# Expert rows of a mixture-of-experts layer: one slot in memory each, or scatters that add into two sums per token

## The chip, the core and the metric

The kernel runs on one core of a Trainium2 chip. Five engines work side by side, each from its own instruction stream, and meet at semaphores: TensorE (PE in the rows; its weight loads are PEld), VectorE (DVE), ScalarE (ACT), GpSimd (POOL) and SyncE (SP), which here issues DMAs. Sixteen DMA engines move the data of all queues. The metric is the time of one execution on the device, in microseconds (us).

## What is computed

The reference is one layer of a streaming encoder for 320 tokens (256 of a new stream, 64 of a running one) with 1024 features, all in float32: a projection, three token mixers, a merge with layer norm, and then a mixture of experts with a second layer norm. The change lies in the mixture of experts:

```python
s = sigmoid(t @ w_router)                 # 320 tokens, 64 experts
eidx = top 8 of (s + router_bias), out of the 4 best of 8 groups
gates = s[eidx] / sum * 2.5
routed = sum over the 8 chosen e: gate * (silu(t @ w1[e]) * (t @ w3[e])) @ w2[e]
h = layer_norm(alpha * h + routed + shared)
```

Each token gets the sum of eight expert rows of 1024 numbers, so there are 320 * 8 = 2560 rows, 40 per expert on average.

## The kernel before

Earlier stages run first: the recurrent mixer (about 130 to 450 us of the span, where the unused DRAM rows of the experts are also cleared), the other mixers, merge, layer norm and routing, up to about 973 us. Then come the experts.

**Experts.** They are handled in 32 pairs (`NP`), experts 2n and 2n+1 in pair n. A pair has 128 rows: 64 places (`CAP`) for each of its two experts, of which about 40 hold a token. For each pair TensorE gathers the token rows by one-hot matrices (`gather`, two halves, L1036 and L1041), or for five of them (`FETCHED`: 6, 11, 16, 21, 26) turns rows that GpSimd has fetched from memory with an indirect DMA (L2352). Then come `hidden` (L1069, 32 matmuls), `turn` (L1077) and `down` (L1088, 16 matmuls). TensorE's order for pair n is: hidden(n), first half of the rows of n+1, turn(n), second half of the rows of n+1, down(n). If an expert had more than 64 tokens, a loop behind `more > 0` would take them; it doesn't run with these inputs.

**VectorE in a pair.** Its order is `hid_step(n)`; `x_step(n+1)`, which copies half of the gathered rows out (L2121) and the row's place (`IDX`); the one-hot matrices of pair n+2; and `y_step(n)` (L1496 on 128x512), which scales half of the expert's output by the gate into `Y`. ScalarE does the other half of each.

**The scatter.** GpSimd's `scatter(n)` waits for both halves of `Y`, issues one indirect DMA (L2340) that stores the 128 rows of 4 KB in DRAM, then waits until it has landed and adds one to `rows_out` (L2344). Only then does it go on to the next. `IDX` and `Y` have two buffers, so `x_step(n+2)` on VectorE waits until scatter n has landed. The row of a token's k-th chosen expert goes to a slot of its own: `slots` has 2560 rows, and a place without a token has an index beyond the end and is not stored. The slot comes from a scan over the chosen experts in the routing stage (`TRK`, L2039 and the lines behind it), which ends in `INFO`, a table of gate and place for each token and expert. The last two pairs (30 and 31) aren't scattered: TensorE adds them by one-hot matrices (`combine`, L1099).

**Weights.** SyncE loads 6.3 MB for each pair, into three slots used in turn. The up weights of pair n (L498, two of 2 MB) are issued when hidden(n-3) is done, the down weights (L501, two of 1 MB) when down(n-3) is.

**The end.** After scatter 29 has landed, SyncE loads all slots, five times 2 MB (L533, L542), over weights that are no longer needed. VectorE sums them (`sum_rows`: adds of 2048, 1024 and 1024 numbers per partition, L244, L246, L249, four times: three between its steps of the last two pairs, one after them). TensorE adds the remaining rows of the last 64 tokens with 16 matmuls (L1155). Then VectorE adds TensorE's sums (L1492), takes the statistics (L2200) and does the layer norm; SyncE stores the output.

## Time and profile before

| | |
|---|---|
| three runs | 1503.83, 1505.06, 1506.80 us |
| median | 1505.06 us |
| span of the profiled execution | 1502.1 us, 2.96 below the median |
| TensorE busy | 1457.5 us (97% of the span) |
| VectorE busy | 647.1 us (43%) |
| GpSimd busy | 116.8 us (8%) |
| DMA moved | 375.27 MB |

The span runs from the first to the last instruction of one execution; no other figure of that execution's time is shown. "Idle before <- X" in a row is time in which the engine waited, and X what ended it. "DMA to landing" is the time from the issue of a transfer to its last byte. Matmul ends are modelled, so matmul rows overlap a little.

### The profile page before, as it was taken

Reading aid. Unit: us, or ns where it says so; the run is one execution under the profiler, and the core shown is the slowest. Engines: PE = TensorE matmul, PEld = TensorE weight load, DVE = VectorE, ACT = ScalarE, POOL = GpSimd, SP = SyncE. Lnnn points to the kernel's source line nnn. Section 1 sums busy time; section 2 is a strip of 40 time slices with the busy share of each in tenths; the row PEclk is TensorE's granted clock in tenths of the full one; section 3 lists DMA queues with packets and bytes.
Section 4 is the critical chain, followed back from the end, with each engine's and each line's share of the span. In section 5 each row is a group of like instructions: output and inputs, shape, how many; then the busy total and the mean of one; then the engine's idle time right before and its main releaser. Section 6 shows DMA issues by size and latency. Waiting matters only on the chain.

```text
span 1502.1 us, 31068 instructions
## 1 busy us (share of the span) xinstructions
PE 1457.5 (97%) x13071; PEld 1011.2 (67%) x13071; DVE 647.1 (43%) x1227; ACT 390.4 (26%) x874; POOL 116.8 (8%) x107
## 2 busy tenths in 40 slices
PE   7999999999999999999999999999999999999995
PEld 6776667677776777767766765766666767675751
DVE  5223778875644677734541114622211112121228
ACT  2112444442322554435431011111111111111111
POOL 3000113121010000000000000000000001000000
PEclk9999999999999999999999999999999999999998
DMA  7778375563344544565577538689999999999985
GB/s 243 168 174 181 101 214 166 132 203 97 103 130 147 138 112 116 178 180 163 135 231 263 157 100 359 251 337 399 417 423 430 428 426 429 426 428 429 427 342 211
DMA packets 157017, 375.27 MB, mean 250 GB/s; under 512 B 101708, under 2 KB 110300, under 8 KB 139216
## 3 DMA queue, kind: packets, MB, share of 16 engines
q1 hardware_dynamic: 123712, 341.35, 63.9%
q10 hardware_dynamic: 26592, 15.49, 3.5%
q0 software_dynamic: 6576, 16.48, 3.2%
q8 instruction: 102, 1.67, 0.5%
q14 instruction: 35, 0.29, 0.1%
HBM read 327.14 MB, written 51.95 MB: 252 GB/s over the span
## 4 chain that ended last, share of the span: by engine, by line
PE 82%; DVE 7%; DMA 4%; ACT 2%; DVEq 2%; issue 1%; SPq 1%; ACTq 1%; POOLq 0%
PE PS L576 27%; PE PS L1069 14%; PE PS L919 8%; PE PS L1036 7%; PE PS L1088 6%; PE PS L624 4%; PE PS L1041 2%; PE PS L957 2%; DVE region L1492 2%; DVE region L1499 2%; PE PS L632 1%; ACT L1172 1%; PE PS L1052 1%; PE PS L1077 1%; PE PS L817 1%
## 5 line engine op out<-in xcount | busy, mean ns | idle before, releaser
L576 PE MATMUL PS<-h0T,region 128*128 128x320 f32 x1808 | 510.2, 437 | 1.0 <-issue 0.8
L576 PEld LDWEIGHTS PS<-h0T,region 128*128 128x128 f32 x1808 | 336.8, 190 | 144.6 <-issue 12.2
L1172 ACT ACTIVATE region<-PS 128x9 f32<-128x9 f32 (+6 forms) x407 | 148.5, 383 | 681.9 <-PE PS L576 311.8
L1069 PE MATMUL PS<-region 128*64 128x512 f32 x1024 | 228.8, 592 | 0.0
L1069 PEld LDWEIGHTS PS<-region 128*64 128x64 f32 x1024 | 124.5, 137 | 92.2 <-issue 31.9
L1492 DVE TENSOR_TENSOR region<-region 128x256 f32<-128x256 f32 (+10 forms) x210 | 127.0, 624 | 96.8 <-ACTq L1218 76.2
L919 PE MATMUL PS<-region 128*128 128x320 f32 x512 | 138.6, 433 | 1.3 <-DMA region<-wo 1.2
L919 PEld LDWEIGHTS PS<-region 128*128 128x128 f32 x512 | 97.0, 190 | 42.5 <-issue 1.7
L1172 ACT ACT_TABLE_LOAD x80 | 102.6, 1283 | 73.1 <-DMA region<-projected 56.7
L1088 PE MATMUL PS<-region,history 128*64 128x512 f32 x512 | 119.7, 596 | 1.0 <-ACTq L1454 0.7
L1172 ACT ACTIVATE region<-region 128x256 f32<-128x256 f32 (+8 forms) x160 | 81.2, 531 | 147.9 <-DMA region<-projected 37.0
L1036 PEld LDWEIGHTS PS<-region,h 128*128 128x128 f32 x864 | 100.6, 192 | 22.5 <-issue 22.4
L1036 PE MATMUL PS<-region,h 128*128 128x128 f32 x864 | 108.1, 278 | 0.4 <-issue 0.4
L1492 DVE TENSOR_TENSOR history<-region,PS 128x256 f32<-128x256 f32 x32 | 13.5, 421 | 200.4 <-ACTq L1449 200.3
L1492 DVE TENSOR_TENSOR region<-PS,region 128x1024 f32<-128x1024 f32 (+3 forms) x49 | 38.2, 807 | 123.1 <-PE PS L919 93.2
L2121 DVE COPY region<-PS 128x512 f32<-128x512 f32 x32 | 22.1, 692 | 157.2 <-PE PS L1052 76.1
L1088 PEld LDWEIGHTS PS<-region,history 128*64 128x64 f32 x512 | 56.1, 137 | 38.5 <-issue 13.7
L2340 POOL DMA_INDIRECT expert_rows<-region,row_index x25 | 24.4, 976 | 721.1 <-DVEq L2149 721.1
L1499 DVE SCALAR_TENSOR_TENSOR region<-region,feature_vectors 128x320 f32<-128x320 f32 (+1 forms) x103 | 65.9, 639 | 19.9 <-ACTq L285 8.3
L1172 ACT ACTIVATE region<-PS,region 128x512 f32<-128x512 f32 x33 | 22.7, 688 | 158.1 <-PE PS L1088 158.0
L624 PEld LDWEIGHTS PS<-region 64*64 64x64 f32 x2720 | 50.0, 134 | 19.1 <-issue 13.4
L624 PE MATMUL PS<-region 64*64 64x64 f32 (+1 forms) x2720 | 56.4, 227 | 6.1 <-DVEq L1690 2.7
(210 smaller groups left out, 1163.8 us busy)
## 6 DMA issues: line engine op xcount, KB each, us to landing
region<-moe_w SPq DMA_DIRECT2D x64, 2048.0 KB, 17.4
region<-moe_w SPq DMA_DIRECT2D x64, 1024.0 KB, 15.0
region<-w_in SPq DMA_DIRECT2D x115, 512.0 KB, 5.6
region<-wo SPq DMA_DIRECT2D x32, 512.0 KB, 3.6
projected<-region ACTq DMA_DIRECT2D x65, 167.5 KB, 3.9
expert_rows<-region SPq DMA_DIRECT2D x20, 512.0 KB, 7.2
region<-expert_rows SPq DMA_DIRECT2D x5, 2048.0 KB, 14.4
region<-projected SPq DMA_DIRECT2D x10, 768.0 KB, 6.3
```

The lines of the kernel that those rows point to most:

```text
L576: last = mm(PS[:, 6 + i % 2, 0:NTOK], WR[:, i, k, :], H0T[:, k, :], start=(k == 0), stop=(k == KT - 1))
L624: last = mm(head(out(j), 1 - x if across and j > 3 else x), head(lhs(j), x), head(rhs(j), x), **kw)
L919: last = mm(PS[:, b, 0:NTOK], WR[:, q, k, :], OT[:, 8 * q + k, :], start=(k == 0 and q < 3), stop=(k == KT - 1 and q != 2))
L957: last = mm(PS[:, 2 * t + h, :], MG[:, k, t * 128:t * 128 + 128], WOUT[:, k, h * 512:h * 512 + 512], start=(k == 0), stop=(k == KT - 1))
L1036: last = mm(bank(h, 4, 128)[:, k], H0[:, t, (4 * h + k) * 128:(4 * h + k) * 128 + 128], OH[:, p, t, :], start=(h == 0 and k == 0 and t == ...
L1041: last = mm(bank(g, 4, 128)[:, k], head(H0, g)[:, 2, (4 * g + k) * 128:(4 * g + k) * 128 + 128], head(OH, g)[:, p, 2, :], start=(g == 1 an ...
L1069: last = mm(PS[tiles(i), 2, :], XE[:, k, tiles(i)], W13[r][i][:, k * 512:k * 512 + 512], start=(k == 0), stop=(k == KT - 1))
L1088: last = mm(PS[tiles(i), 5 + h, :], HIDT[:, f, tiles(i)], W2[r][i][:, f * D + h * 512:f * D + h * 512 + 512], start=(f == 0), stop=(f == 1))
L1172: return nc.scalar.activation(out, in_, f, **kw)
L1492: return dve.tensor_tensor(out, a, b, op)
L1499: return dve.scalar_tensor_tensor(out=out, in0=a, scalar=s, in1=b, op0=op0, op1=op1)
L2340: pool.indirect_dma_start(slots[:, :], bass.IndirectOffsetOnAxis(ap=places, axis=0), Y[:, p, :], None, bounds_check=last_slot, oob_is_err= ...
```

## The change

The DRAM tensor of 2560 slots becomes one of 640 rows: two sums for each token. Experts with an even number go to row `token`, those with an odd number to row `320 + token`. The two experts of a pair thus never meet in a row within one scatter. Each scatter now has `compute_op=ALU.add`: it adds its rows to what stands there. Its place in the instruction streams and its waits stay.

- The 20 stores that clear the slots become 5, all issued behind the weights of the first step of the recurrent mixer.
- The routing stage no longer counts a token's chosen experts; the place is the token's number plus 0 or 320.
- At the end there are two loads of 1 MB and two of 256 KB; VectorE does two adds for each of three token tiles (`add_sums`: 1024 numbers per partition, and 512 in the last tile).
- TensorE's 16 matmuls of L1155 (eight in the program, each of which the trace shows twice) and their wait are gone.

```diff
-SLOTS = NTOK * TOPK
+SUMS = 2 * NTOK
...
-        slots = nc.dram_tensor("expert_rows", (SLOTS, D), FP32, kind="Internal").ap()
+        sums = nc.dram_tensor("expert_sums", (SUMS, D), FP32, kind="Internal").ap()
+        sums_of = sums.rearrange("(r n) d -> n r d", r=2)
...
-        def sum_rows(e, k):
-
-            t, w = k // 2, 128 if k < 4 else 64
-            rw = ROWS[k][0:w]
-            e.tensor_tensor(rw[:, 0:2], rw[:, 0:2], rw[:, 2:4], ALU.add)
-            e.drain()
-            e.tensor_tensor(rw[:, 0], rw[:, 0], rw[:, 1], ALU.add)
-            e.drain()
-            if t < 2:
-                e.tensor_tensor(ACC[:, t, :], ACC[:, t, :], rw[:, 0], ALU.add)
-            else:
-                e.tensor_copy(ROWS[k][64:128, 0, 0:512], rw[:, 0, 512:D])
+        def add_sums(e, t):
+
+            acc = ACC[:, t, :] if t < 2 else ACC[:, 2, 0:512]
+            for r in range(2):
+                e.tensor_tensor(acc, acc, ROWS[t][:, r], ALU.add)
                 e.drain()
-                e.tensor_tensor(ACC[:, 2, 0:512], ACC[:, 2, 0:512], ROWS[k][:, 0, 0:512], ALU.add)
-            return e.drain()
 
...
-            def clear_rows(c):
-                for a in range(7 * c, min(7 * c + 7, SLOTS // 128)):
-                    sp.dma_start(slots[a * 128:a * 128 + 128, :], ZERO).then_inc(sem("slots_zero"), 16)
+            def clear_sums(zero):
+                for a in range(SUMS // 128):
+                    sp.dma_start(sums[a * 128:a * 128 + 128, :], zero).then_inc(sem("sums_zero"), 16)
...
-                clear_rows(c)
-            sp.wait_ge(sem("slots_zero"), 16 * (SLOTS // 128))
+                if c == 0:
+                    clear_sums(ZERO)
+            sp.wait_ge(sem("sums_zero"), 16 * (SUMS // 128))
...
+            def rows_in(t):
+                if t < 2:
+                    sp.dma_start(ROWS[t], sums_of[t * 128:t * 128 + 128]).then_inc(sem(f"rows_in{t}"), 16)
+                    return
+                for h in range(2):
+                    sp.dma_start(head(ROWS[2], h), sums_of[256:NTOK, :, 512 * h:512 * h + 512]).then_inc(sem("rows_in2"), 16)
 
             sp.wait_ge(sem("pair_done"), SENT)
             sp.wait_ge(sem("rows_out"), SENT + 2)
-            for k in range(4):
-                if k == 3:
-                    sp.wait_ge(sem("pair_done"), SENT + 1)
-                rows_in(k)
-            rows = slots[2048:SLOTS, :].rearrange("(p k) d -> p k d", k=4)
-            sp.dma_start(ROWS[4], rows).then_inc(sem("halves_in"), 16)
+            for t in range(TT3):
+                rows_in(t)
...
-            combine(2, 1)
-            pe.wait_ge(sem("halves_in"), 16)
-            for k in range(4):
-                for h in range(2):
-                    last = mm(head(PS, h)[:, back[2][h], :], E, ROWS[4][:, k, h * 512:h * 512 + 512], start=False, stop=(k == 3))
-            last.then_inc(sem("tokens"), 1)
+            combine(2, 1, False, True).then_inc(sem("tokens"), 1)
...
-            for t in range(TT3):
-                dve.tensor_tensor_scan(TRK[:, t], CHO[:, t], CON[:, C_ONE:C_ONE + NE], 0.0, add, mul)
+            for r in range(2):
+                ts(INFO[:, :, 1 + 2 * r:2 * NE:4], wide(VEC[:, V_TOK8:V_TOK8 + TT3].unsqueeze(2), NE // 2), 0.125,
+                   float(NTOK * r - SKIP), mul, add)
             dve.drain()
             dve.tensor_reduce(CNT3, TIE3, AX.X, add)
-            stt(INFO[:, :, 1:2 * NE:2], TRK, -1.0 - SKIP, wide(VEC[:, V_TOK8:V_TOK8 + TT3].unsqueeze(2), NE), add, add)
-            ts(CNT, VEC[:, V_TOK8 + 2:V_TOK8 + 3], -0.5, 1024.0, mul, add)
-            dve.drain()
-            ts(TRK[:, 2], TRK[:, 2], 4.5, 252.0, ALU.is_gt, mul)
-            dve.drain()
-            stt(INFO[:, 2, 1:2 * NE:2], TRK[:, 2], CNT, INFO[:, 2, 1:2 * NE:2], add, add)
+            dve.drain()
             ts(CNT3, CNT3, 1e-30, None, mx)
             dve.wait_ge(sem("shared_silu"), 1)
             tt(SHID, SHID, PS[:, 6:8, 0:NTOK], mul)
...
+            def add_rows(t):
+                dve.wait_ge(sem(f"rows_in{t}"), 16 if t < 2 else 32)
+                add_sums(dve, t)
...
                 if n == NP - 2:
                     turned_back(1)
                     add_rows(0)
+                if n == NP - 1:
                     add_rows(1)
-                if n == NP - 1:
-                    add_rows(2)
                 if n != NP - 2:
                     y_step(n, n % 2)
-            add_rows(3)
+            add_rows(2)
...
-                pool.indirect_dma_start(slots[:, :], bass.IndirectOffsetOnAxis(ap=places, axis=0),
-                                        Y[:, p, :], None, bounds_check=last_slot, oob_is_err=False
+                pool.indirect_dma_start(sums[:, :], bass.IndirectOffsetOnAxis(ap=places, axis=0),
+                                        Y[:, p, :], None, bounds_check=last_sum, oob_is_err=False, compute_op=ALU.add
                                         ).then_inc(sem(f"rows_sent{p}"), 16)
                 pool.wait_ge(sem(f"rows_sent{p}"), m * 16 + 16)
                 nc.gpsimd.sem_inc(sem("rows_out"), 1)
```

On VectorE in the routing stage, from the mask that clears the unused token rows to the multiply for the shared expert (`h0T`); `history` holds the scan's result, which the listing prints as SCALAR_TENSOR_TENSOR. Before, and then now:

```order
L1492 TENSOR_TENSOR region<-region 128x192
L2039 SCALAR_TENSOR_TENSOR history<-region,constants 128x64 x3
L2041 TENSOR_REDUCE region<-region 128x3
L1499 SCALAR_TENSOR_TENSOR region<-history,feature_vectors 128x192
L1495 TENSOR_SCALAR region<-feature_vectors 128x1
L1495 TENSOR_SCALAR history<-history 128x64
L1499 SCALAR_TENSOR_TENSOR region<-history,region 128x64
L1496 TENSOR_SCALAR region<-region 128x3
L1492 TENSOR_TENSOR h0T<-h0T,PS 128x640 [waits shared_silu]
```

```order
L1475 TENSOR_TENSOR region<-region 128x192
L1478 TENSOR_SCALAR region<-feature_vectors 128x96 x2
L2025 TENSOR_REDUCE region<-region 128x3
L1479 TENSOR_SCALAR region<-region 128x3
L1475 TENSOR_TENSOR h0T<-h0T,PS 128x640 [waits shared_silu]
```

Three scans and four further operations on the places make way for two.

On VectorE at the end, from the first sum of loaded rows on; `silu_ready` is that of pair 31, `pair_done` its down projection. Before (two adds of the last sum follow), and then now:

```order
L244 TENSOR_TENSOR region<-region 128x2048 [waits rows_in0]
L246 TENSOR_TENSOR region<-region 128x1024
L249 TENSOR_TENSOR region<-region 128x1024
L244 TENSOR_TENSOR region<-region 128x2048 [waits rows_in1]
L246 TENSOR_TENSOR region<-region 128x1024
L249 TENSOR_TENSOR region<-region 128x1024
L1492 TENSOR_TENSOR history<-region,PS 128x256 [waits silu_ready]
L244 TENSOR_TENSOR region<-region 128x2048 [waits rows_in2]
L246 TENSOR_TENSOR region<-region 128x1024
L249 TENSOR_TENSOR region<-region 128x1024
L1496 TENSOR_SCALAR region<-PS,region 128x512 [waits pair_done]
L244 TENSOR_TENSOR region<-region 128x2048 [waits rows_in3]
```

```order
L246 TENSOR_TENSOR region<-region 128x1024 [waits rows_in0]
L246 TENSOR_TENSOR region<-region 128x1024
L1475 TENSOR_TENSOR history<-region,PS 128x256 [waits silu_ready]
L246 TENSOR_TENSOR region<-region 128x1024 [waits rows_in1]
L246 TENSOR_TENSOR region<-region 128x1024
L1479 TENSOR_SCALAR region<-PS,region 128x512 [waits pair_done]
L246 TENSOR_TENSOR region<-region 128x512 [waits rows_in2]
L246 TENSOR_TENSOR region<-region 128x512
```

Twelve adds become six. One group still stands behind `pair_done`, and before the first of pair 31's steps there is one group where there were two.

On SyncE at the end, after the loads of the norm's vectors. Before, and then now:

```order
L525 DMA h0T<-lnv 128x1024
L533 DMA region<-expert_rows 128x4096 [waits rows_out,pair_done]
L533 DMA region<-expert_rows 128x4096 x2
L533 DMA region<-expert_rows 128x4096 [waits pair_done]
L542 DMA region<-expert_rows 128x4096
```

```order
L519 DMA h0T<-lnv 128x1024
L523 DMA region<-expert_sums 128x2x1024 [waits rows_out,pair_done]
L523 DMA region<-expert_sums 128x2x1024
L526 DMA region<-expert_sums 64x2x512 x2
```

The wait for the scatters (`rows_out`) stands ahead of all of these loads in both.

## Rows read from the trace of the kernel before

**Rows 1.** The page, 40 slices of the span: DMA share in tenths.

```profile
...
DMA  7778375563344544565577538689999999999985
...
```

**Rows 2.** Timeline, one pair: start, us, engine line op out<-in [idle before <-releaser].

```profile
1411.36 7.17 PE L1069 MATMUL PS<-region 128*64 128x512 f32 x32
...
1424.20 3.63 PE L1088 MATMUL PS<-region,history 128*64 128x512 f32 x15
...
1424.55 0.69 DVE L2121 COPY region<-PS 128x512 f32<-128x512 f32 x1 [5.12 <-POOLq L2344]
...
1425.50 1.07 DVE L1496 TENSOR_SCALAR region<-constants,region 128x64 f32<-128x64 f32 x6
1427.87 0.75 DVE L1496 TENSOR_SCALAR region<-PS,region 128x512 f32<-128x512 f32 x1 [1.30 <-PE PS L1088]
```

**Rows 3.** Timeline of POOL: the first scatter and the last two.

```profile
991.47 1.07 POOL L2340 DMA_INDIRECT expert_rows<-region,row_index  x1 [376.06 <-DVEq L2149]
...
1429.49 0.97 POOL L2340 DMA_INDIRECT expert_rows<-region,row_index  x1 [15.20 <-DVEq L2149]
1446.58 0.97 POOL L2340 DMA_INDIRECT expert_rows<-region,row_index  x1 [16.12 <-DVEq L2149]
```

**Rows 4.** By line: scatters, all and 1227 to 1430; who waited; fetches.

```profile
DMA to landing us min/median/max: 6.9/10.1/13.2
...
DMA to landing us min/median/max: 10.1/10.6/13.2
...
  DVE region L2121: 69.5, 14
...
DMA to landing us min/median/max: 10.9/11.6/12.4
```

**Rows 5.** Stretch 1413 to 1429 (last: DMA share, GB/s); queue q0, 1417.3 to 1418.3.

```profile
1413.00:1429.00 16.00, 16.00 (x112) 11.49 (x110) 3.06 (x11) 2.05 (x4) 0.97 (x1) 1.00 1.01 428
...
q0 software_dynamic: 24, 0.10, 23.9%
```

**Rows 6.** By line: landing of up weights (L498), issued at 997 and 1418.

```profile
DMA to landing us min/median/max: 9.5/11.7/14.0
...
DMA to landing us min/median/max: 19.6/23.2/26.8
```

**Rows 7.** Timelines of the routing stage, VectorE and then TensorE.

```profile
955.22 0.65 DVE L2039 TENSOR_TENSOR_SCAN history<-region,constants 128x64 f32<-128x64 f32 x3
...
957.25 0.81 DVE L1492 TENSOR_TENSOR h0T<-h0T,PS 128x640 f32<-128x640 f32 x1
...
959.25 0.52 DVE L1495 TENSOR_SCALAR region<-region 128x128 f32<-128x128 f32 x3
...
958.33 8.97 PE L1020 MATMUL PS<-region,h0T 128*128 128x512 f32 x24 [1.07 <-DVEq L2052]
```

**Rows 8.** Timeline of the end of the kernel.

```profile
1453.95 8.41 SPq L533 DMA_DIRECT2D region<-expert_rows  x4
...
1464.35 1.23 DVE L246 TENSOR_TENSOR region<-region 128x1024 f32<-128x1024 f32 x1
...
1477.43 0.75 DVE L1496 TENSOR_SCALAR region<-PS,region 128x512 f32<-128x512 f32 x1
...
1478.27 4.71 PE L1099 MATMUL PS<-region 128*128 128x512 f32 x12 [0.39 <-DVEq L2149]
1478.30 2.29 DVE L244 TENSOR_TENSOR region<-region 128x2048 f32<-128x2048 f32 x1
...
1482.81 3.60 PE L1155 MATMUL PS<-region,constants 128*64 128x512 f32 x16
...
1483.27 1.22 DVE L1492 TENSOR_TENSOR region<-region,PS 128x1024 f32<-128x1024 f32 x1
...
1484.60 1.29 DVE L2200 BATCH_NORM_STATS2 region<-region 128x6 f32<-128x512 f32 x2
```

**Rows 9.** What SP waited for behind the zero stores.

```profile
SPq L336 <- DMA expert_rows<-region: 10.5, 1, 10.5
```

More of the change, by code:

```diff
@@ L206, in hybrid_layer @@
         W2 = [[v[:, 4096:6144] for v in pair] for pair in slot]
-        ROWS = [shaped(REGION[:, (24576 if k < 3 else 0) + k % 3 * 4096:][:, 0:4096], 4, D) for k in range(6)]
+        ROWS = [shaped(REGION[:, 24576 + 2 * D * t:][:, 0:(2 * D if t < 2 else D)], 2, D if t < 2 else D // 2)
+                for t in range(TT3)]
         assert mixer_base + 24 * NTOK <= mixer_end
@@ L525, in _ @@
                 sp.dma_start(LN2[:, k, :], io['lnv'][4 + k:5 + k, :].to_broadcast([128, D])).then_inc(sem("ln_in"), 16)
-            def rows_in(k):
-                t = k // 2
-                if k < 4:
-                    rows = slots[t * 1024:t * 1024 + 1024, :].rearrange("(p k) d -> p k d", k=8)[:, k % 2 * 4:k % 2 * 4 + 4, :]
-                else:
-                    rows = slots[2048 + (k - 4) * 256:2304 + (k - 4) * 256, :].rearrange("(p k) d -> p k d", k=4)
-                sp.dma_start(ROWS[k][0:128 if k < 4 else 64], rows).then_inc(sem(f"rows_in{k}"), 16)
+            def rows_in(t):
[4 more added lines that the diff above has]
+                    sp.dma_start(head(ROWS[2], h), sums_of[256:NTOK, :, 512 * h:512 * h + 512]).then_inc(sem("rows_in2"), 16)
             sp.wait_ge(sem("pair_done"), SENT)
             sp.wait_ge(sem("rows_out"), SENT + 2)
-            for k in range(4):
-                if k == 3:
-                    sp.wait_ge(sem("pair_done"), SENT + 1)
-                rows_in(k)
-            rows = slots[2048:SLOTS, :].rearrange("(p k) d -> p k d", k=4)
-            sp.dma_start(ROWS[4], rows).then_inc(sem("halves_in"), 16)
+            for t in range(TT3):
+                rows_in(t)
             with sp.If(more > 0):
                 sp.wait_ge(sem("cleared"), 1)
-                for a in range(SLOTS // 128):
-                    sp.dma_start(slots[a * 128:a * 128 + 128, :], ROWS[0][:, 0, :]).then_inc(sem("slots_zero"), 16)
-                sp.wait_ge(sem("slots_zero"), 16 * (SLOTS // 128) * 2)
+                clear_sums(ROWS[0][:, 0, :])
+                sp.wait_ge(sem("sums_zero"), 16 * (SUMS // 128) * 2)
                 with sp.Fori(0, NP) as m:
@@ L554, in _ @@
                 sp.wait_ge(sem("rows_out"), NP * NBLK + 2)
-                for k in range(6):
-                    rows_in(k)
+                for t in range(TT3):
+                    rows_in(t)
             for k, t in enumerate((1, 0)):
@@ L2154, in turned_back @@
                 dve.drain().then_inc(sem("turned_back"), 1)
-            def add_rows(k):
-                dve.wait_ge(sem(f"rows_in{k}"), 16)
-                sum_rows(dve, k)
+            def add_rows(t):
+                dve.wait_ge(sem(f"rows_in{t}"), 16 if t < 2 else 32)
+                add_sums(dve, t)
             onehot(1, 1, 0)
@@ L2225, in _ @@
                         y_step(n, b % 2)
-                for k in range(6):
-                    dve.wait_ge(sem(f"rows_in{k}"), 32 if k < 4 else 16)
-                    sum_rows(dve, k)
+                for t in range(TT3):
+                    dve.wait_ge(sem(f"rows_in{t}"), 32 if t < 2 else 64)
+                    add_sums(dve, t)
                 for t in range(TT3):
@@ L2329, in _ @@
             meet(pool, 4)
-            last_slot = pool.to_reg(SLOTS - 1)
+            last_sum = pool.to_reg(SUMS - 1)
             def scatter(m, p, n):
@@ L2344, in scatter @@
                 nc.gpsimd.sem_inc(sem("rows_out"), 1)
-            pool.wait_ge(sem("slots_zero"), 16 * (SLOTS // 128))
+            pool.wait_ge(sem("sums_zero"), 16 * (SUMS // 128))
             def fetch_rows(k):
@@ L2363, in _ @@
                 nc.gpsimd.sem_inc(sem("rows_out"), 2)
-                pool.wait_ge(sem("slots_zero"), 16 * (SLOTS // 128) * 2)
+                pool.wait_ge(sem("sums_zero"), 16 * (SUMS // 128) * 2)
                 with pool.Fori(0, NP // 2 * (NBLK - 1)) as m:
```

## The prediction

> **What bounds the kernel now.** I read the page first. TensorE is busy for 97% of the span, and in the expert stage (the last third) the DMA share is at nine tenths or more too [rows 1]. So that stage has two limits close together. The stretches show how close: from 1413 to 1429 us TensorE is busy in all 16 of 16 us, and the DMA engines have a share of 1.01 at 428 GB/s [rows 5]. TensorE's own work sets the pace, but nothing is free beside it.
>
> Next comes the scatter, since the change is there. The timeline of one late pair shows VectorE's copy of the gathered rows (L2121) idle for 5.12 us and released not by TensorE but by POOL's semaphore, the landing of the scatter before last [rows 2]. This happened 14 times, 69.5 us in all [rows 4]. TensorE didn't wait for it: the copy is needed only in the middle of the next hidden stage. But it says that the scatter's landing has almost no room left. The scatters land 6.9 to 13.2 us after their issue, 10.1 in the median, and 10.6 in the second half of the stage [rows 4].
>
> The end of the kernel was read last. There VectorE, not TensorE, carries the chain: it sums the loaded rows until 1483.2 and only then adds TensorE's result [rows 8].
>
> **What it costs if a scatter lands later.** The scatters form a loop through VectorE. Scatter n lands; the copy starts (1424.55); copy and one-hot matrices end at 1426.57, 2.02 us later; the gated write takes 0.75; from its end (1428.62) to the next issue (1429.49) it is 0.87 [rows 2, 3]. With 0.1 from landing to copy that is 3.75 us. So two issues can't be closer than landing time + 3.75. The first and the last of 30 scatters are issued at 991.47 and 1446.58 [rows 3], 15.69 us apart on average. A landing time of 15.69 - 3.75 = 11.9 us can therefore be carried for ever; above it every pair gets longer by the excess. Ahead of that stands one stock: the copy may be late, once, until the middle of the next hidden stage. That is 3.6 us of down (1424.20 to 1427.83) plus half of 7.17, less 1.0 for the copy itself, so 6.2; I count 5, for what is rough in matmul ends [rows 2].
>
> **The price of adding in memory** isn't in the trace. At the lower end it is 0: the transfer has as many packets and rows as before, and its time is mostly turns among the weights' packets. A gain is excluded, as nothing gets less. At the upper end it is 11.6 us: the median landing of a fetch of 128 rows from memory (L2352) [rows 4], if the old rows were read first and stored only then. The nearest row is that same fetch, as it also reads memory under the same load: it lands 1.5 us later than the median scatter. It moves 8 rows per DMA engine, a scatter about 5. A row of 4 KB takes 0.159 us on one engine (24 packets, 23.9% of 16 engines in 1 us) [rows 5]. So I take off 3 rows (0.5) and put on the 5 old rows that must now be read (0.8): 1.5 - 0.5 + 0.8 = **1.8 us** more.
>
> The Trainium skill speaks against this change as well: "Collectives: The Full Stack", in the section on the bandwidth ceiling and the fold count, has a reduce step at about half a copy's rate, since each chunk has two reads and the addition itself is free. By it each row would cost one more read of the same length, an estimate of 0.8 us for 5 rows, and the loop below would still just hold; no row here shows an adding transfer.
>
> Then 10.6 + 1.8 = 12.4, which is 0.5 over 11.9. The first six pairs land faster and are spaced wider, so 24 pairs count: 12 us, less the stock of 5, is 7. Stepping through the 30 pairs with their own landing times gives 9, because five pairs, the fetched ones, are some 3 us shorter, and landings go up to 13.2. I take **+8**. What is queued behind the copy on VectorE is the one-hot matrices and the gated write; TensorE waits for the copied rows, GpSimd for the write.
>
> **More bytes.** Reading 80 rows per pair costs all 16 engines 80 x 0.159 / 16 = 0.79 us per pair. The up weights' slower landing rose from 14.0 to 26.8 us through the stage [rows 6], so the DMA engines already fall behind. Those weights are needed some three pairs less one hidden stage after the issue, 3 x 15.7 - 7.2 = 40 us: a margin of 13 at the end. Some 23 pairs with extra 0.79 use up 18 of it: 5 us over in the worst case, nothing if a part of the reads finds room. This is not added to the +8: a pace stretched by 8 us gives the transfers that time. The larger of the two counts.
>
> **The end.** Four sums of 2.29 + 1.23 + 1.23 us and gaps go [rows 8]; six adds of 1.23, or about 0.7 for 512 numbers, come, one group of which is behind the last gated write. That write starts at 1477.43 and would have started 0.36 earlier without adds ahead of it; TensorE waited 0.39 for it. Its combine stage then starts at 1477.9, the first four matmuls (of 4.71 for twelve) are over at 1479.5, and VectorE's first addition starts at 1479.6 instead of 1483.27: **-3.6**. The last adds of 512 fit between 1477.9 and 1479.4. The later additions follow at 1.22 + 1.29 each [rows 8], later than TensorE delivers now that L1155 (3.60) is gone, so that removal pays no more. The loads start when scatter 29 has landed (1453.95 before [rows 8], 1.8 and the delay of the pace later now). They are needed by about 1466, when the sums of tile 0 must start so as not to hold pair 31; 2.5 MB instead of 10 has 10 us for that.
>
> **Routing.** Between 955.22 and the multiply at 957.25 stand 2.0 us of work [rows 7]. Now it is two operations (0.17 each by the 0.52 for three), the reduction of 0.35 and small ones, 1.0 with gaps. TensorE waited 1.07 us for this chain [rows 7], so all of it counts: **-1.0**.
>
> **Clearing.** 15 stores of 512 KB go. SyncE waited 10.5 us for them once [rows 9]; in that stretch no other engine waited for a load that stood behind, TensorE carries the chain, so 0; at most -10.5. The order of SyncE's loads changes nowhere else that anyone waits.
>
> **Sum.** 1502.1 - 3.6 - 1.0 + 8 = 1505.5 us of span. The median of the runs is 2.96 above the span, and I keep that: 1508.5 us. The change is then slower by 0.2%.
>
> **Rivals.**
> 1. *The loop holds.* The landing grows by at most 1.2 us, because the reads run ahead of the stores or hide in the turns of the weights' packets. For it: the last scatter, with little beside it, takes 6.9 us for the same rows, so bytes are a small part of landing. Against it: 14 waits already. It gives 1505.06 - 4.6 = 1500.5, up to 1505 if the weights' 5 us come due. This is the faster side; the point where it decides is a median landing of 11.9 us.
> 2. *Adding is slow.* Landing grows by 3 us or more, since a DMA engine is held up by each row. By the loop, 3 us give (13.6 - 11.9) x 24 - 5 = 36, hence 1536; 5 us give 84, hence 1584. The loop makes it steep. Against it: the fetch, which reads memory too, is only 1.5 slower.
> 3. *The weights come late*, landings within bounds: 5 us of TensorE waiting in the last pairs, 1505.
>
> **Chances.** A change of 0.2%, 3 us, is about what a measurement can tell from none. Forecast (extra landing 1.2 to 3, time 1502 to 1536) 0.40; rival 1 0.27; rival 3 0.10; rival 2 0.23. Rival 1 and the gentlest end of the forecast are faster by over 3 us: 0.30. The rest of the forecast's low end and rival 3 are within 3 us: 0.22. Slower: 0.48. The range goes from 1499.5, a clean gain, to 1560, which leaves out the steep half of rival 2.
>
> **What would show it.** Landing of the scatters: 12.4 in the median of the second half. The wait of L2121's copy for POOL's semaphore: more than 20 times. TensorE's hidden stage waiting for VectorE's copy in late pairs, some 8 us in all, and the spacing of scatters 15.95 instead of 15.69. At the end, the first addition to TensorE's sums right behind its first four matmuls; in routing, TensorE's wait of 1.07 gone. If TensorE waits for weights instead, rival 3 was right. If the median landing stays under 11.9, I am wrong on the sign; if it is near 14, on the size by tens of us.

## The result, and the profile after

The changed kernel takes 1525.13 us in the median of four runs (1518.04 to 1526.37), the kernel before 1505.12 (1503.83 to 1506.80) beside it: a ratio of 1.0131, interval 1.0106 to 1.0156. It is slower by about 20 us. The span of its profiled execution is 1522.2 us, against 1502.1.

The page of the changed kernel, first the busy times, then two of the rows by slices, then the queues (packets, MB, share of the time of 16 DMA engines):

```profile
PE 1462.0 (96%) x13055; PEld 1003.2 (66%) x13055; DVE 633.8 (42%) x1216; ACT 390.2 (26%) x874; POOL 134.9 (9%) x107
...
DMA  7778364343345445564676558599999999999972
GB/s 236 172 170 186 95 182 115 89 128 95 108 116 159 114 112 160 172 190 115 190 257 205 150 186 353 218 379 390 408 407 406 405 410 401 403 411 403 406 277 71
...
q1 hardware_dynamic: 121664, 325.62, 60.4%
q0 software_dynamic: 6576, 16.48, 4.8%
```

VectorE has less to do and the DMA engines move 16 MB less. But in the expert stage, where the DMA share stands at nine tenths as before [rows 1], they now move 401 to 411 GB/s; before, 428 [rows 5].

**Where the 20 us are.** Three marks of the trace cut the span: the first scatter, the start of pair 31's hidden stage (the last one), and the end.

| us | before | after | difference | forecast |
|---|---|---|---|---|
| start to first scatter | 991.47 | 990.85 | -0.6 | -1.0 |
| to last hidden stage | 470.35 | 488.79 | +18.4 | +8 |
| to the end | 40.3 | 42.6 | +2.3 | -3.6 |

In the runs below the first scatter stands anywhere from 987.1 to 992.9 us, also where nothing ahead of it was changed. So the first row tells little, and a stretch is better counted from its own first scatter than from the start.

**The scatter.** Its line, over all 30, and over the second half of the stage (1236 to 1450):

```profile
L2318 POOL DMA_INDIRECT expert_sums<-region,row_index x25: 1547/1549/1712, 990.9 to 1466.1; - x25
L2318 POOL DMA_INDIRECT expert_sums<-region,fetched_places x5: 1549/1584/1585, 1088.6 to 1417.2; - x5
...
DMA to landing us min/median/max: 10.1/12.4/15.4
```

```profile
DMA to landing us min/median/max: 11.2/12.4/14.9
```

Before it was 6.9/10.1/13.2 and, late, 10.1/10.6/13.2 [rows 4]. An adding scatter lands 2.3 us later, in the median of all, and 1.8 later in the second half. A part of that is the issue itself: it is counted in, and lasts 1.55 us where it lasted 0.97. The first 4 KB row starts 4.65 us after the start of the issue instead of 4.12 (medians of the packets in the trace).

**Who waits.** From 985 us to the end, the waits of the changed kernel (us in total, times, longest):

```profile
DVE region L2100 <- POOLq L2322: 252.7, 27, 13.6
...
PE PS L1057 <- DVEq L2104: 6.9, 4, 2.4
...
PE PS L1065 <- DVEq L2123: 5.7, 6, 3.7
PE PS L1057 <- DVEq L2118: 5.3, 3, 2.7
...
PE PS L1057 <- DMA region<-moe_w: 0.6, 2, 0.4
```

The copy of the gathered rows (L2100; L2121 before) waits for the landing before last in 27 pairs instead of 14 [rows 4], for 9.66 us in one late pair where it was 5.12 [rows 2]:

```profile
1411.92 7.17 PE L1057 MATMUL PS<-region 128*64 128x512 f32 x32
...
1413.50 0.69 DVE L2100 COPY region<-PS 128x512 f32<-128x512 f32 x1 [9.66 <-POOLq L2322]
...
1415.63 0.75 DVE L1479 TENSOR_SCALAR region<-PS,region 128x512 f32<-128x512 f32 x1
1417.24 1.55 POOL L2318 DMA_INDIRECT expert_sums<-region,fetched_places  x1 [13.58 <-DVEq L2128]
```

By these rows the loop through VectorE is the bound, and weights are not: TensorE waits 0.6 us for them. The second half of that reading says too much: the weights have no room left. These are the up weights of the last pair (L492), from issue to landing, and the hidden stage that needs them:

```profile
L492 SPq DMA_DIRECT2D region<-moe_w x2: 340/424/507, 1435.3 to 1435.7; - x2
...
DMA to landing us min/median/max: 19.6/31.7/43.8
```

```profile
1479.64 7.09 PE L1057 MATMUL PS<-region 128*64 128x512 f32 x32
```

1435.7 + 43.8 = 1479.5: the hidden stage starts 0.14 us after its weights. Before it was 26.8 us [rows 6]; those of the last pair, issued at 1418.9, were there at 1445.8, 16.0 us before they were needed. Over the stage of the changed kernel this margin shrinks from 29 us (pair 5) over 9.4 (pair 20) to 0.7 (pair 28). So the loop makes nearly all of the delay in this kernel, and at its end the weights are just as late: two limits meet, and each hides the other's wait. The experiments take them apart.

The delay is not spread evenly. From one hidden stage to the next it is mostly 16.17 us, before as after, and before it was about 12.6 ahead of a fetched pair. Of the 31 spacings five grow by 2.1 to 4.6 us, those that begin at pairs 13, 16, 18, 21 and 26; no other grows by more than 0.8. And the waits are not all of it. TensorE waits 15.9 us in the stretch from the first scatter to the last hidden stage where it waited 3.3, 12.6 of the 18.4 us. Twice, behind waits of 2.67 and 2.27 us, the granted clock is at its lower level (1.2 of 2.4 GHz) for 3.4 us, from 1270.0 and 1317.8 on; before, it stays at the upper one in this stage. The hidden stages, before and then now (busy us, mean ns):

```profile
L1069 PE MATMUL PS<-region 128*64 128x512 f32 x1024 | 228.8, 592 | 0.0
```

```profile
L1057 PE MATMUL PS<-region 128*64 128x512 f32 x1024 | 234.0, 601 | 12.8 <-DVEq L2104 6.9
```

**The end.** Timeline of the changed kernel:

```profile
1476.12 3.65 PE L1076 MATMUL PS<-region,history 128*64 128x512 f32 x16
...
1478.39 0.92 SPq L523 DMA_DIRECT2D region<-expert_sums  x2
...
1490.97 2.53 DVE L246 TENSOR_TENSOR region<-region 128x1024 f32<-128x1024 f32 x2 [11.22 <-DMA region<-expert_sums]
1493.58 0.42 DVE L1475 TENSOR_TENSOR history<-region,PS 128x256 f32<-128x256 f32 x1
...
1494.09 0.44 PE L1065 MATMUL PS<-constants,history 128*128 128x128 f32 x2 [3.73 <-DVEq L2123]
...
1495.02 5.35 PE L1076 MATMUL PS<-region,history 128*64 128x512 f32 x16 [0.50 <-ACTq L1437]
```

The last scatter, issued at 1466.09, takes 12.2 us (6.9 before). The loads of the sums go out then, and land after 12.6. VectorE's two additions for them stand ahead of the hidden step of pair 31 in its stream, so this step, whose input is ready a little after 1487, comes at 1493.58, and TensorE waits 3.73 us. Over 1491 to 1500 the granted clock is 0.81, a mean of its two levels, 2.4 and 1.2 GHz, and the 16 matmuls of down take 5.35 us; in the pair before they took 3.65.

### The profile page after: what moved, and what is told of

It reads as the page before. It is cut to its first block, busy times and chain, and to the rows that moved or that the text cites. A ratio compares the mean times of both kernels' runs of the same rounds, so it can differ in the third digit from the quotient of the medians.

```text
span 1522.2 us, 31002 instructions
## 1 busy us (share of the span) xinstructions
PE 1462.0 (96%) x13055; PEld 1003.2 (66%) x13055; DVE 633.8 (42%) x1216; ACT 390.2 (26%) x874; POOL 134.9 (9%) x107
## 3 DMA queue, kind: packets, MB, share of 16 engines
q0 software_dynamic: 6576, 16.48, 4.8%
HBM read 319.28 MB, written 44.08 MB: 239 GB/s over the span
## 4 chain that ended last, share of the span: by engine, by line
PE 57%; DMA 25%; DVE 10%; issue 3%; DVEq 2%; ACT 1%; ACTq 1%; POOLq 0%; SPq 0%
PE PS L564 26%; DMA expert_sums<-region,row_index 18%; PE PS L907 9%; DMA expert_sums<-region,fetched_places 5%; PE PS L612 3%; DVE region L1479 3%; DVE region L1475 2%; DVE region L1482 2%; PE PS L1057 2%; PE PS L945 2%; DVE region L2100 1%; PE PS L1024 1%; PE PS L967 1%; PE PS L620 1%; ACT L1155 1%
## 5 line engine op out<-in xcount | busy, mean ns | idle before, releaser
L564 PEld LDWEIGHTS PS<-h0T,region 128*128 128x128 f32 x1808 | 336.8, 190 | 144.2 <-issue 12.4
L1155 ACT ACTIVATE region<-PS 128x9 f32<-128x9 f32 (+6 forms) x407 | 148.5, 383 | 698.2 <-PE PS L564 311.8
L1057 PE MATMUL PS<-region 128*64 128x512 f32 x1024 | 234.0, 601 | 12.8 <-DVEq L2104 6.9
L1057 PEld LDWEIGHTS PS<-region 128*64 128x64 f32 x1024 | 116.8, 138 | 118.5 <-issue 48.0
L2100 DVE COPY region<-PS 128x512 f32<-128x512 f32 x32 | 22.1, 692 | 274.3 <-POOLq L2322 252.7
L1155 ACT ACTIVATE region<-region 128x256 f32<-128x256 f32 (+8 forms) x160 | 81.1, 530 | 145.7 <-DMA region<-projected 37.2
L2318 POOL DMA_INDIRECT expert_sums<-region,row_index x25 | 39.0, 1561 | 723.6 <-DVEq L2128 723.6
L1155 ACT ACTIVATE region<-PS,region 128x512 f32<-128x512 f32 x33 | 22.7, 688 | 159.8 <-PE PS L1076 159.7
L612 PEld LDWEIGHTS PS<-region 64*64 64x64 f32 x2720 | 49.6, 134 | 18.5 <-issue 12.3
```

What stands on the lines that cost most here:

```text
L564: last = mm(PS[:, 6 + i % 2, 0:NTOK], WR[:, i, k, :], H0T[:, k, :], start=(k == 0), stop=(k == KT - 1))
L612: last = mm(head(out(j), 1 - x if across and j > 3 else x), head(lhs(j), x), head(rhs(j), x), **kw)
L1057: last = mm(PS[tiles(i), 2, :], XE[:, k, tiles(i)], W13[r][i][:, k * 512:k * 512 + 512], start=(k == 0), stop=(k == KT - 1))
L1155: return nc.scalar.activation(out, in_, f, **kw)
L2100: dve.tensor_copy(XE[:, 4:8], bank(1, 4, 128))
L2318: pool.indirect_dma_start(sums[:, :], bass.IndirectOffsetOnAxis(ap=places, axis=0), Y[:, p, :], None, bounds_check=last_sum, oob_is_err=Fa ...
```

## The experiments

Each result is given as a ratio to the kernel before on the same chip. "Landing" is the mean over the 30 scatters; "last hidden" the start of pair 31's hidden stage, and "from the first scatter" the time from the issue of the first scatter to it, 470.35 us before.

### The change without the addition

```diff
-  Y[:, p, :], None, bounds_check=last_sum, oob_is_err=False, compute_op=ALU.add
+  Y[:, p, :], None, bounds_check=last_sum, oob_is_err=False
```

> The changed kernel with its scatters storing instead of adding (what lands last stands in a sum, so routed rows of a token are lost; all else is as changed). My theory, that the price is in the adding: landing back at 10.1 us in the median, hidden of the last pair about 18 us earlier than in the changed kernel, and the end 3.6 us shorter than before, so about 1500.5 us, 0.3% faster than before. The rival, that the smaller target (640 rows written again and again instead of 2560 once) or the loads at the end make it slow: 1515 to 1525 us.

Measured: 1498.47 us, ratio 0.9966 (0.9954 to 0.9979), landing 10.1, the last one 6.9; last hidden at 1461.1, from there to the end 36.9 us (40.3 before). All that the addition does not touch is therefore worth -4.4 us, as the sum said (-3.6 and -1.0), and from the first scatter it is 470.1 us. The line of the scatter, and VectorE's wait:

```profile
L2318 POOL DMA_INDIRECT expert_sums<-region,row_index x25 | 24.4, 977 | 719.7 <-DVEq L2128 719.7
```

```profile
DVE region L2100 <- POOLq L2322: 72.8, 14, 7.6
```

977 ns per issue instead of 1549, and 14 waits of the copy as before. The whole loss is the price of `compute_op`. Packets (6576), bytes and even the page's count of bytes read from memory (319.28 MB) are the same with and without it; what differs is the time of the packets.

### The addition alone, in the kernel before

```diff
-  Y[:, p, :], None, bounds_check=last_slot, oob_is_err=False
+  Y[:, p, :], None, bounds_check=last_slot, oob_is_err=False, compute_op=ALU.add
```

> The kernel before with its scatters adding into its cleared slots, the only difference. If adding is the whole price: landing 12.4 us in the median, and 18 us or more on top of before, about 1524 to 1530 us (the long end of before stays). The rival, that repeated writes to the same rows are what is slow: about 1505 us, as before.

Measured: 1536.96 us, ratio 1.0219 (1.0202 to 1.0236), landing 12.1, last hidden at 1482.06 (+20.2; from the first scatter +18.8). The addition costs about the same in 2560 slots that are each hit once as in 640 sums: it is no matter of rows that several experts share. The end is 14.6 us longer than before, since the 10 MB of loads start after a later last scatter and VectorE's sums hold up the last hidden step (TensorE waits up to 11.9 us for it).

### A late landing without a byte more

The signal of the landing is held back on GpSimd by 12 small clears (the gap from landing to the next issue goes from 3.8 to 6.8 us), in the kernel before.

```diff
                 pool.wait_ge(sem(f"rows_sent{p}"), m * 16 + 16)
+                for _ in range(12):
+                    pool.memset(PAD[:, :], 0.0)
+                    pool.drain()
                 nc.gpsimd.sem_inc(sem("rows_out"), 1)
```

> The kernel before with some 2 us of small clears on GpSimd between the landing of a scatter and its signal: no byte more is moved. The theory of the loop (landing + 3.75 us can't be longer than the spacing of 15.7 us) gives +12 us for 2 us of delay, +20 for 2.4, +34 for 3. The rival, that the changed kernel is slow because the DMA engines have more to carry and the weights come late, gives no more than 2 us here.

Measured: 1523.69 us, ratio 1.0140 (1.0123 to 1.0157); last hidden at 1477.07 (+15.3; from the first scatter +16.3). Its waits:

```profile
DVE region L2122 <- POOLq L2347: 245.9, 28, 12.4
```

That is the picture of the changed kernel, without its bytes. The expectation was too high because the landings themselves fell to 9.0 us in the mean; 9.0 + 3.0 = 12.0 is the effective landing. In the next run, with the same clears but hardly slower than before, they are 10.4, so the clears don't shorten them; the slower pace does. How is not shown: the DMA share from 1100 to 1430 us is 1.01 in both.

The same with three buffers for the places and gates, so that VectorE's copy waits for one scatter less:

```diff
+                g = n % 3
-                dve.wait_ge(sem("rows_out"), n + 1)
+                dve.wait_ge(sem("rows_out"), n)
...
-                    ts(IDX[:, p:p + 1], PS[:, 4, 1:2], float(SKIP), None, add)
+                    ts(IDX[:, g:g + 1], PS[:, 4, 1:2], float(SKIP), None, add)
...
+                dve.wait_ge(sem("rows_out"), n + 1)
+                ts(Y[:, p, 0:512], PS[:, 5, :], GA[:, g:g + 1], None, mul)
-                ts(Y[:, p, 0:512], PS[:, 5, :], GA[:, p:p + 1], None, mul)
```

> The kernel before, its scatters' signals 3.0 us late as in b_late, and with three buffers for places and gates, so VectorE's copy doesn't wait for the scatter before last. If b_late's 20.8 us came from the loop through that copy, they go: within 3 us of before, 1501 to 1506. If a late signal costs for another reason (the gated write, the fetches behind the scatters), 10 us or more stay.

Measured: 1505.49 us, ratio 1.0023 (1.0012 to 1.0033), last hidden at 1457.77, which is 470.4 us from the first scatter, as before. Of 20.8 us of loss 3.1 are left, and they are at the end. That settles the loop: it is a cause by itself, and it runs through the copy's wait.

### The changed kernel without the loop

The same three buffers in the changed kernel.

> The changed kernel with three buffers instead of two for the row places and the gates, so that VectorE's copy for pair n+2 no longer waits for scatter n (its gated write does). If the loop is the cause, most of the 18 us of the expert stage come back; the rest of the time depends on whether the weights now come late, 0 to 5 us. 1501 to 1508 us. The rival, that the adding scatters load the DMA engines too much: TensorE waits for weights instead, 1515 us or more.

Measured: 1525.73 us, ratio 1.0155 (1.0138 to 1.0172). Nothing is gained: from the first scatter it is 488.9 us, where the changed kernel has 488.8. The loop is gone, and TensorE waits for weights:

```profile
PE PS L1057 <- DMA region<-moe_w: 13.2, 7, 4.5
```

Their landing time climbs to 44 us by the middle of the stage and stays there, since no more than three pairs can be ahead. The theory that the loop alone explains the loss falls here. From the first scatter, the loop alone costs 16.3 us (the late landing above), the weights alone 18.5, both together 18.4: they don't add up.

### Bytes without the addition

Three buffers, the plain scatter of the kernel before, and in 29 pairs one more load of 328 KB that nothing uses.

```diff
+                if n > 3:
+                    sp.wait_ge(sem("extra_in"), 16 * (n - 3))
+                sp.dma_start(HT[:, 1024:1664], io['moe_w'][n, :, 0:640]).then_inc(sem("extra_in"), 16)
```

> The kernel before with three buffers and plain scatters, and behind the down weights of each of 29 pairs one load more of 128 x 640 numbers (328 KB, as much as the old rows that an adding scatter reads) that nobody uses. If the DMA engines' time for the old rows is what holds the changed kernel with three buffers, TensorE waits for weights: 0.78 us more transfer per pair, 23 us in all, against a margin of 13 to 16: 5 to 10 us slower than before; 15 us or more if the margin is smaller than I think. If bytes don't matter (the adding itself holds an engine up), no more than 2 us.

Measured: 1525.17 us, ratio 1.0150 (1.0132 to 1.0168). Most of the time is not where it was expected. Last hidden is at 1467.05, 5.2 us late, or 7.5 from the first scatter: that is inside the 5 to 10 us foreseen for the stage. The other 15.6 us are at the end, where this edit holds back SP's loads of the rows; they say nothing of the change. The stretch from 1100 to 1430 us, queues q1 (weights) and q0 (scatters, fetches): the kernel before, the changed one, the one with extra loads:

```profile
q1 hardware_dynamic: 12081, 132.37, 94.2%
q0 software_dynamic: 3456, 8.39, 6.5%
```

```profile
q1 hardware_dynamic: 11491, 125.51, 89.9%
q0 software_dynamic: 3328, 8.12, 11.3%
```

```profile
q1 hardware_dynamic: 14314, 132.10, 94.4%
q0 software_dynamic: 3456, 8.39, 6.5%
```

Adding packets take 11.3% of the engines' time for slightly fewer bytes than took 6.5%: 4.8% of 330 us in 20 pairs, 0.79 us of all engines per pair, just what the prediction had. (By the shares of the whole span, 4.8% of 1522.2 us less 3.2% of 1502.1, it is 25 us, 0.83 per pair.) The extra load takes the same 0.77 (328 KB at 428 GB/s). Yet from the first scatter the one costs 18 us and the other 7.5. The last up weights tell why, set against the hidden stage that needs them:

| us | last up weights issued | landed | last hidden stage |
|---|---|---|---|
| before | 1418.9 | 1445.8 | 1461.82 |
| change without addition | 1418.2 | 1445.2 | 1461.10 |
| extra loads | 1437.7 | 1464.5 | 1467.05 |
| every second scatter adds | 1422.1 | 1463.5 | 1465.01 |
| changed | 1435.7 | 1479.5 | 1479.64 |
| changed, three buffers | 1434.0 | 1477.8 | 1477.92 |
| addition alone | 1438.9 | 1481.9 | 1482.06 |

Where all scatters add, the last hidden stage starts 0.1 to 0.2 us after its weights. The kernel before had 16.0 us in hand. The first scatters of these kernels stand up to 4 us apart, so I count the landings from there: extra loads delay the last weights by 21 us, additions in every second scatter by 17, all additions by 34. 21 - 16 = 5 and 17 - 16 = 1 are roughly the delays seen (7.5 and 2.4). 34 - 16 = 18 is no such test, as those hidden stages start with their weights; it only gives the size. Over 30 scatters that is 1.1 us for each addition, not 0.79.

### Every second scatter adds

Only the scatters of even pairs have `compute_op`.

```diff
+                how = {} if isinstance(n, int) and n % 2 else dict(compute_op=ALU.add)
-  Y[:, p, :], None, bounds_check=last_sum, oob_is_err=False, compute_op=ALU.add
+  Y[:, p, :], None, bounds_check=last_sum, oob_is_err=False, **how
```

> The changed kernel with only the scatters of even pairs adding, those of odd pairs storing (part of the routed rows is lost). Both limits have a point from which they bind: landings alternate between 12.4 and 10.1, 11.2 in the mean, under the 11.9 that the loop carries, and the added transfer is 12 us in all, inside the weights' margin. So far less than half of the 20 us: 1499 to 1504, about before's time or better. A price in proportion to the adding scatters, with no such point, gives 1498.5 + 13 = 1512.

Measured: 1503.72 us, ratio 1.0002 (0.9991 to 1.0012), landing 11.3, last hidden 3.9 us later than without additions, where all additions cost 18.5 (from the first scatter 2.7 and 18.7). Half the additions cost a fifth or less: this is a limit that is passed, not a price per scatter. Both limits give that. 11.3 is under what the loop can carry, and half of 34 is about the 16 us in hand.

### Which places the rows have

If a place belongs to a fixed DMA engine, the rows may load some engines more than others, and the weights wait for the fullest. First the places of each pair's second expert are filled from the end (`CON[:, C_REV...]` is the row 63, 62, ... 0), in the changed kernel with three buffers and in the kernel before:

```diff
-                        ts(OH[:, p, t, 64 * i:64 * i + 64], CON[:, C_IOTA + CAP * b:C_IOTA + CAP * b + CAP],
+                        ts(OH[:, p, t, 64 * i:64 * i + 64],
+                           CON[:, C_REV:C_REV + CAP] if i == 1 and b == 0 else CON[:, C_IOTA + CAP * b:C_IOTA + CAP * b + CAP],
```

> a_three with the 64 places of the second expert of each pair filled from the end (a reversed row of numbers for its one-hot matrices); same rows, bytes and packets. a_three's expert stage was 16 us longer, b_bytes' 5 us with as many bytes, and a load's landing counts from the slowest DMA engine. If that gap is uneven work (both experts' places 0 to 39 fall on the same engines), landings get shorter than 12.3 and the weights come earlier: 5 to 10 us faster than a_three (1.0155 of before), a ratio near 1.010. If adding holds up each engine by itself, nothing changes: 1.0155.

> The kernel before with the second expert's places filled from the end. Its TensorE has no wait to lose, so the time stays within 2 us of before under both theories; if the work of the DMA engines is uneven, the up weights' landing at the end of the stage falls from 26.8 to 20 us or so, and the scatters' median from 10.1 to 9.5.

Measured: ratios 1.0155 (1.0130 to 1.0179) and 1.0001 (0.9989 to 1.0012): no effect in either. The 5 to 10 us were not there, and in the kernel before the last up weights take 28.7 us to land (26.8 without the edit, about 20 expected).

Then, with both experts, rank r goes to place 8 x (r mod 8) + r / 8 (and the later sums of the next section):

```diff
+    c[:, C_REV:C_REV + CAP] = np.arange(CAP).reshape(8, CAP // 8).T.ravel()
```

> The changed kernel with three buffers for the scatter's places, the later sums at the end, and the places of an expert's tokens dealt out one after another over the eight groups of eight places (token rank r of both experts goes to place 8 x (r mod 8) + r / 8, by a permuted constant), so that each group has about 5 of 40 rows instead of five groups having 8 and three none. It is to be held against the same kernel with the second expert's places reversed, which takes 1.0111 of the kernel before, with scatters landing in 12.2 us on the mean, up weights of the last pair landing 43.9 us after their issue, and the last hidden stage starting at 1476.2. Theory A: places are given to the DMA engines in groups of eight neighbours, the adding rows then fall on some engines only, and the weights' last bytes wait for the fullest engine. Then a landing falls to 8 to 10 us, the last up weights land some 10 us earlier, and the ratio is 1.000 to 1.004. Theory B: which place a row has does not matter to the engines, or only their total counts: landings 12.2, ratio 1.011 as before. Theory C: places go to engines in turn (place modulo 16); then this order is the uneven one, since ten engines get all the rows: landings 13 to 15, ratio above 1.015.

Measured: 1532.91 us, ratio 1.0201 (1.0181 to 1.0222), against 1.0111 with the reversed places (the last run below); landing 12.7, last hidden at 1492.5. TensorE's wait for weights, and the stretch from 1100 to 1430 us (TensorE busy, ..., granted clock, DMA share, GB/s):

```profile
PE PS L1059 <- DMA region<-moe_w: 23.5, 13, 4.6
```

```profile
1100.00:1430.00 330.00, 306.96 (x1924) 186.03 (x1921) 54.58 (x184) 39.86 (x78) 34.32 (x23) 0.98 1.00 391
```

So the places do matter, in the direction of theory C: all transfers together get 391 GB/s instead of 406 with the same rows and bytes, and this order leaves six of sixteen residues of the place nearly empty. That agrees with places dealt to the engines in turn. But it isn't enough: by that rule the reversed order is the most even one, and it gained nothing. Which engine gets which place stays open.

### The later sums, and all together

VectorE adds the loaded sums of tile 0 behind the hidden step of pair 31, those of tile 1 behind its gated write.

```diff
                 if n == NP - 2:
                     turned_back(1)
-                    add_rows(0)
                 if n == NP - 1:
-                    add_rows(1)
+                    add_rows(0)
...
+            add_rows(1)
             add_rows(2)
```

> The changed kernel, its first addition of sums moved from ahead of VectorE's hidden step of the last pair to behind it, and the second one behind the last gated write. TensorE's wait of 3.7 us for that step goes, and the slower matmuls behind it; the gated write is no longer late: 4 to 5 us faster than the changed kernel, about 1519 to 1520 (against its 1525 and 1502.9 of before here). If the loads of the sums are late for all of it, no gain: 1524.

Measured: 1519.33 us, ratio 1.0112 (1.0087 to 1.0136); from the last hidden stage to the end 39.1 us instead of 42.6. Its timeline:

```profile
1486.84 0.38 PE L1065 MATMUL PS<-constants,history 128*128 128x128 f32 x2
1487.49 2.53 DVE L246 TENSOR_TENSOR region<-region 128x1024 f32<-128x1024 f32 x2 [3.23 <-DMA region<-expert_sums]
1487.71 3.65 PE L1076 MATMUL PS<-region,history 128*64 128x512 f32 x16 [0.50 <-ACTq L1437]
```

TensorE no longer waits, and down takes 3.65 us again.

> The adding kernel with all that seemed to help: three buffers, the second expert's places from the end, and the first additions of sums behind the last hidden step. By the parts: 1.0155 less 4 us for the end less what a_three_rev brings; 1.003 to 1.013. It would beat before only if nearly the whole expert stage came back (its end alone is 3.6 us shorter).

Measured, with three buffers, reversed places and later sums: 1518.65 us, ratio 1.0111 (1.0088 to 1.0133), no better than the later sums alone. No version with all the additions came near the kernel before.

## Why the prediction was right, and where it was wrong

The sign and the range held (1499.5 to 1560), the size did not: 1508.5 us foreseen, 1525 measured, 3 us slower against 20. The sign was a close call, with a chance of 0.48 for slower, and the range was wide enough for either.

**The price of adding: right in number, in part by luck.** Landing in the second half: 12.4 us foreseen, 12.4 measured. But the sum of 1.8 us knew nothing of the longer issue, which alone puts the first row 0.5 us later. The reasoning, that each row costs one more read of its length, holds in the engines' time in the steady stretch: q0's share goes from 3.2% of the span to 4.8% for the same 6576 packets and 16.48 MB. This is the rule of the Trainium skill ("Collectives: The Full Stack", bandwidth ceiling and fold count: a reduce step has two reads per chunk, and the addition itself is free), and the trace agrees in size: 0.79 us more per pair, as by the 0.159 us of one row [rows 5]. That the extra time is a read is not shown, as the page counts no more bytes read. And the last scatter doesn't fit: with the engines less than half busy, its packets take 16.5% of their time over 12.3 us where they took 11.6% over 7.0, which is 0.40 us for each of 78 rows instead of 0.16.

**The loop: right in kind, too small.** Copy waiting more than 20 times (27), TensorE waiting for the copy, spacing wider: all there. Alone it is worth 16 us, by the late signal, where I had 8. The step that failed is the pace. I took the mean spacing of all 30 scatters, 15.69. But the first four intervals are wider: 68.2 us in sum, before as after. The other 25 stood 15.48 apart before and 16.29 after. 15.48 - 3.75 leaves 11.7 us to carry, not 11.9, and the mean landing in these 25 is 12.55, since the four issued right behind a fetch take 13.6 to 15.4. 12.55 + 3.74 is the 16.29 measured. (This sum alone proves nothing: with three buffers, where no copy waits for the loop, landing and spacing also differ by 3.73. The proof is the late signal.) 0.81 x 25 = 20.3. The stage lost 18.4, so a stock of about 2 would close the sum, not 5; it is what is left over, not a measurement. Nor does "every pair gets longer by the excess" hold: five spacings took nearly all of it, and some of it is the lower clock behind the waits, which the sum didn't have.

**The weights: wrong step.** "The larger of the two counts" was the right rule, and "a margin of 13" was near (16.0 at the last pair, 12.5 at pair 26). The extra was wrong: 18 us foreseen at most, 34 measured. 0.79 per pair gives 24 over 30 pairs, not 18 over 23. The other 10 or so don't show as busy time of the engines. They show at the end of the weights, where the engines don't finish together. The mean DMA share in stretches of 4 us of the changed kernel:

| stretch | 1454-1458 | 1458-1462 | 1462-1466 | 1466-1470 | 1470-1474 | 1474-1478 |
|---|---|---|---|---|---|---|
| DMA share | 0.99 | 0.86 | 0.59 | 0.72 | 0.40 | 0.27 |

The last up weights land at 1479.5, some 20 us after the first engines run dry. In the kernel before the share falls from 0.93 (1438 to 1442) over 0.78 to 0.56 (1446 to 1450). I had reckoned with the mean of the engines; a load of weights is there when the last of them is. What makes some later than others is open. It was shown that the order of places can make the kernel slower (+0.9%), not that the order in use is the reason. Rival 3 was thus half right, with three times its price, and the loop at almost the same length hid it from the row that should have shown it.

**The end: wrong.** Foreseen -3.6, measured +2.3. Without additions it is -3.4, so the removal of the four sums and of L1155 was sized well. The step that failed is "2.5 MB instead of 10 has 10 us for that". The last scatter, with stragglers of the weights beside it, took 12.2 us where 6.9 + 1.8 was in my mind, so the loads went out at 1478.4 and not near 1464; and I didn't ask what on VectorE is queued behind the wait for them. It is the hidden step of the last pair. Moving it recovers 3.5.

**Routing: right.** TensorE's wait of 1.07 [rows 7] is gone, and from the mask that clears the unused rows to the multiply for the shared expert it is 1.35 us instead of 2.31, so -1.0. The -0.6 of the table also holds how the earlier stages differ from run to run. **Clearing:** no gain is seen, as forecast; no run tests it by itself. The kernel without additions has -4.4 for all of them.

## What to carry to other kernels

A margin has to be read against the pace of the steady stretch, not against a mean that includes the slower first rounds; and where the loop and the DMA engines both stand near their limit, an extra cost of 0.8 us per round should be put to each of them separately. The absence of a wait for a resource doesn't show that it has room: compare the landing with the start of the work that needs it. Three buffers in place of two take such a loop out, but that gains nothing until the second limit is gone too; an addition done by the DMA took 0.8 us more of all engines per 80 rows here. Whether it pays beside idle engines no run shows, and the last scatter (12.2 us instead of 6.9 beside engines less than half busy) speaks against taking it for granted.

## What the hardware showed that was not expected

- An adding scatter also costs more at its issue: GpSimd is busy for 1549 ns instead of 977.
- Slowing the kernel shortened the landings (10.1 to 9.0 us in the mean, 10.4 in a kernel with the same clears that kept its pace), so a landing is not a constant to which a delay can be added.
- After TensorE's wait of 3.73 us at the end, the granted clock was 0.81 over the next stretch (3.4 us at its lower level); without that wait it stayed at 1.00 (1487 to 1496) in the kernel with later sums:

```profile
1491.00:1500.00 9.00, 5.42 (x18) 1.79 (x20) 5.29 (x5) 0.38 (x1) 0.00 (x0) 0.81 0.02 9
```

```profile
1487.00:1496.00 9.00, 8.46 (x32) 2.90 (x32) 6.69 (x7) 4.47 (x5) 0.00 (x0) 1.00 0.05 15
```

- The order of the rows among the 128 places, with nothing else changed in what is moved, took 15 GB/s of 406 from the expert stage.
